# A decoder trunk step: all 576 tokens together against two groups of 288 that pass the layers out of step

## The chip, the cores and the metric

The kernel runs on one core of one Trainium2 chip. A core has TensorE (PE, the matmul array, with PEld for its weight loads), VectorE (DVE), ScalarE (ACT), GpSimd (POOL) and SyncE (SP), which here issues the DMAs. Each engine takes its instructions in program order, and the engines meet through semaphores. The metric is the device time of one execution in microseconds (us).

## The reference

Two layers, each of three sub-layers with a norm before and after, on 512 prompt tokens (one sequence) and 64 sample tokens (8 sequences of 8) that share the weights. Model width 1024, hidden width 2816, all in float32.

```python
def layer(x, ...):
    x = x + 0.5 * rmsnorm(swiglu(rmsnorm(x, pre0), gate0, up0, down0), post0)
    m, h_last, new_conv, S_fin = mixer(rmsnorm(x, pre1), ...)
    x = x + rmsnorm(m, post1)
    x = x + 0.5 * rmsnorm(swiglu(rmsnorm(x, pre2), gate1, up1, down1), post2)

def mixer(h, ...):
    xl, yl, q, k, v, g, gd = split(h @ w_in)
    xc = causal_conv(xl, width 4)                       # carries 3 rows along the sequence
    hl = rg_lru(xc)                                     # h_t = a_t*h_(t-1) + b_t, gates from 64x64 blocks
    lru_out = rmsnorm(hl * gelu(yl), lru_norm)
    gk = log_sigmoid(gd @ w_gate + b) / 16
    o, S = gla(q, k, v, gk)                             # 4 heads, chunks, state S carried on
    gla_out = rmsnorm(o, gla_norm) * silu(g)
    return concat(lru_out, gla_out) @ w_out
```

Outputs are the tokens after two layers, and the recurrence, convolution and attention states of both kinds of sequence.

## The kernel before

Activations lie transposed in SBUF: 128 channels on the partitions, 8 tiles of channels, 576 tokens along a row (`NT`), of which each matmul takes a half of 288 (`H`). A weight matrix is cut into *units*: one output tile of 128 channels with all its inputs, (128 x 1024) for gate, up, w_in and w_out and (128 x 1408) for down, whose 22 input tiles go in two chunks of 11.

Float32 products are made of three passes of the short format fp32r. ACT rounds a weight unit to `wh` (line 624), DVE forms the rest `wl` = raw - wh (line 823), and PE adds wh·xh + wh·xl + wl·xh (line 373). The operands have the same two parts: `hh` and `hl`, or `hidh` and `hidl` for the hidden layer.

There are two slots (0 and 1) of raw, wh and wl and two of PSUM (`psU`). SP loads the next unit into `raw` when DVE is done with the last (`lo_ready`). `out_taken` tells PE that DVE has emptied a slot of PSUM. Every unit does both halves of the tokens, so each weight is loaded from HBM and split once.

A feed-forward sub-layer goes: gate unit, up unit; DVE takes the gate times the norm's factor `rstd` (line 896), ACT makes the silu (693), POOL multiplies by `rstd` (1232), DVE takes the up product times that (904), ACT rounds it to `hidh` (695) and POOL makes `hidl` (1234). After each chunk the 8 down units follow. Sums of squares over the channels are made by ACT (square), POOL (line 1207, `ssum`) and PE, which sums over the partitions in columns (431); ACT takes a root, DVE a reciprocal and a diagonal (840), and PE spreads it over the partitions (439). Then DVE scales the result (873), adds it to x (878) and makes the next `hl` (846), with ACT's `hh` (641) between.

In the mixer, each of 4 tiles of the recurrence takes four units of w_in, with convolution, gates and scan on DVE and ACT between them. Then come 4 chunks of 128 prompt tokens and one of 64 sample tokens of the attention. Chunks follow one another with no unit of a weight between: exponents (DVE 998), keys (DVE 1014), queries (POOL 1244), scores (PE 490 to 500), placing by masks (DVE 1032, 1044), outputs (PE 512, 523), state (PE 529, 539; DVE 1051 to 1065). Then the norms of the mixer (PE 431, 598) and its output as operand (DVE 1123 to 1131, ACT 795, POOL 1287), and w_out.

Each engine's program is written out by hand, with hardware loops over units, tiles, chunks and layers. One thing follows another for all 576 tokens.

Of the kernel before, what the change touches and what calls it, by code (L numbers as in the profile page):

```python
# [39 lines left out]
NTC = NT // TC  # L55
# [10 lines left out]
V_XC, V_D, V_ONE, V_B, V_AH, V_BS, V_A0, V_H, V_O = 4, 5, 6, 7, 8, 9, 10, 11, 12  # L66
A_R, A_I, A_TAU, A_AA, A_L1, A_L2, A_M, A_GE = range(1, 9)
P_HEAD, P_IX, P_ST = 1, 2, 3

G_SC, G_S, G_KEM, G_S1, G_S2 = 1, 2, 2, 3, 4  # L70
D_N, D_E, D_VC = 1, 2, 3
A_VT, A_KET, A_O = 1, 2, 3
T_VT, T_KE, T_SA, T_SB, T_O, T_SU = range(1, 7)


class Tally:

    def __init__(self, small_step=None):  # L80
        self.small_step, self.count, self.open, self.pauses = small_step, {}, [], 0

    def pause(self):


        if self.small_step:
            self.small_step(self.pauses)
            self.pauses += 1

    def now(self, sem, more=0):  # L90
        v = self.count.get(sem.name, 0) + more
        for reg, rises in self.open:
            if rises.get(sem.name, 0):
                v = reg * rises[sem.name] + v
        return v

    def up(self, sem, k=1):
        self.count[sem.name] = self.count.get(sem.name, 0) + k
        return self.now(sem)

    @contextmanager
    def loop(self, eng, times, rises):
        before = dict(self.count)
        with eng.Fori(0, times) as i:
            self.open.append((i, rises))
            yield i
            self.open.pop()
        rise = {k: v - before.get(k, 0) for k, v in self.count.items() if v != before.get(k, 0)}
        assert all(rises.get(k) == v for k, v in rise.items()), f"a loop raises {rise}, said {rises}"
        for k, v in rise.items():  # L110
            self.count[k] = before.get(k, 0) + v * times

# [25 lines left out]
def halves(ap):  # L138
    return ap.rearrange("p (a n) -> p a n", a=2)
# [1253 lines left out]
```

## Time and profile before

| what | us |
|---|---|
| median of the 3 runs shown | 2519.77 |
| the 3 runs | 2513.7, 2519.77, 2522.1 |
| span of the profiled execution, first to last instruction | 2507.5 |
| median less span | 12.3 |
| PE busy | 2306.2 (92%) |
| DVE busy | 1015.1 (40%) |
| ACT busy | 750.0 (30%) |
| POOL busy | 588.7 (23%) |
| mean granted TensorE clock | 0.939 |
| moved by DMA | 180.67 MB, mean 72 GB/s |

The page gives the span of the profiled execution; that execution has no separate time beside it, so the 12.3 us between the span and the median stand for what lies around it. Busy shares are averages over stages. A busy PE is not PE at full rate, since the ends of matmuls are modelled and overlap; the rate is read from a dense stretch, by count.

### The profile page before, as it was taken

How to read it: one execution, taken by the hardware profiler on the slowest of the kernel's cores; microseconds unless marked ns; L12 is line 12 of the kernel's file. 1: busy time of each engine (PE TensorE's matmuls, PEld its weight loads, DVE VectorE, ACT ScalarE, POOL GpSimd, SP SyncE). 2: the span in 40 equal slices, each digit the busy share in tenths (PEclk: the TensorE clock that was granted, in tenths of full speed). 3: DMA queues.
4: the chain of work that ended last, by engine and by line, in shares of the span. 5: the costliest groups of instructions: out<-in, count | busy, mean ns of one | idle time of the engine just before them, and what ended most of it. 6: DMA issues, size and time to landing. Idle time of an engine off the chain costs nothing.

```text
span 2507.5 us, 43035 instructions
## 1 busy us (share of the span) xinstructions
PE 2306.2 (92%) x16980; PEld 2261.6 (90%) x16980; DVE 1015.1 (40%) x1202; ACT 750.0 (30%) x967; POOL 588.7 (23%) x424
## 2 busy tenths in 40 slices
PE   6999999799678999999879999997996879999997
PEld 6999999699577999999879999996985779999997
DVE  4332332655845422233353223326557453322333
ACT  4221222365423321122232212223653232212221
POOL 3220222221222321122222202222112232201221
PEclk9999999899768999999989999998997689999998
DMA  3222222022011222222112222221220112222221
GB/s 127 84 92 68 84 90 80 26 91 84 0 36 67 68 84 93 72 79 91 54 59 84 95 71 78 93 78 35 80 75 3 51 51 77 86 90 75 81 89 63
DMA packets 48604, 180.67 MB, mean 72 GB/s; under 512 B 5617, under 2 KB 7697, under 8 KB 48017
## 3 DMA queue, kind: packets, MB, share of 16 engines
q1 hardware_dynamic: 48528, 179.63, 22.2%
q8 instruction: 52, 0.85, 0.1%
q14 instruction: 24, 0.19, 0.0%
HBM read 174.74 MB, written 4.87 MB: 72 GB/s over the span
## 4 chain that ended last, share of the span: by engine, by line
PE 82%; issue 6%; DVE 5%; POOL 2%; ACT 2%; DVEq 1%; SPq 0%; DMA 0%; ACTq 0%; POOLq 0%
PE psU L373 79%; DVE hl L846 1%; POOL hl L1287 1%; DVE xT L878 1%; POOL ssum L1207 1%; PE psM L439 1%; DVE sc L1032 1%; PE psM L512 1%; DVE dec L998 1%; PE psM L562 1%; PE psM L431 1%; DVE tmp L873 0%; PE psM L523 0%; POOL qf L1244 0%; PE psU L529 0%
## 5 line engine op out<-in xcount | busy, mean ns | idle before, releaser
L373 PE MATMUL psU<-hh,wh 128*128 128x288 f32 x3712 | 815.5, 302 | 82.1 <-DVE hl L846 45.1
L373 PE MATMUL psU<-hh,wl 128*128 128x288 f32 x3712 | 807.1, 300 | 0.0
L373 PE MATMUL psU<-hl,wh 128*128 128x288 f32 x3712 | 806.7, 299 | 0.0
L624 ACT ACTIVATE wh<-raw 128x1024 fp32r<-128x1024 f32 (+1 forms) x296 | 334.4, 1130 | 1261.9 <-PE psU L373 1261.9
L373 PEld LDWEIGHTS psU<-hh,wh 128*128 128x128 f32 x3712 | 610.0, 192 | 97.8 <-issue 72.2
L373 PEld LDWEIGHTS psU<-hh,wl 128*128 128x128 f32 x3712 | 610.4, 192 | 0.0
L373 PEld LDWEIGHTS psU<-hl,wh 128*128 128x128 f32 x3712 | 609.8, 192 | 0.0
L823 DVE TENSOR_TENSOR wl<-raw,wh 128x1024 fp32r<-128x1024 f32 (+1 forms) x296 | 402.9, 1362 | 134.6 <-ACT wh L624 133.8
L1232 POOL TENSOR_TENSOR actr<-act,rstd 128x576 f32<-128x576 f32 x88 | 168.2, 1912 | 664.0 <-ACT act L693 642.2
L373 PE MATMUL psU<-hidh,wh 128*128 128x288 f32 x1408 | 302.3, 296 | 0.0
L373 PE MATMUL psU<-hidl,wh 128*128 128x288 f32 x1408 | 302.2, 296 | 0.0
L373 PE MATMUL psU<-hidh,wl 128*128 128x288 f32 x1408 | 302.1, 296 | 0.0
L1234 POOL TENSOR_TENSOR hidl<-hid,hidh 128x576 f32 x88 | 158.3, 1799 | 396.2 <-ACT hidh L695 389.3
L1207 POOL TENSOR_TENSOR ssum<-ssum,sq 128x576 f32<-128x576 f32 x92 | 152.8, 1661 | 349.1 <-ACT sq L659 155.3
L373 PEld LDWEIGHTS psU<-hidh,wh 128*128 128x128 f32 x1408 | 227.4, 189 | 0.0
L373 PEld LDWEIGHTS psU<-hidl,wh 128*128 128x128 f32 x1408 | 227.4, 188 | 0.0
L373 PEld LDWEIGHTS psU<-hidh,wl 128*128 128x128 f32 x1408 | 227.4, 188 | 0.0
L904 DVE TENSOR_TENSOR hid<-psU,actr 128x576 f32<-128x576 f32 x88 | 66.7, 758 | 351.4 <-PE psU L373 342.3
L896 DVE TENSOR_TENSOR gate<-psU,rstd 128x576 f32<-128x576 f32 x84 | 63.7, 758 | 324.2 <-PE psU L373 324.2
L930 DVE COPY yT<-psU 128x576 f32 (+1 forms) x32 | 24.2, 758 | 189.3 <-PE psU L373 189.3
L932 DVE TENSOR_TENSOR yT<-psU,yT 128x576 f32 (+1 forms) x32 | 24.2, 758 | 173.0 <-PE psU L373 173.0
L846 DVE SCALAR_TENSOR_TENSOR hl<-xT,par,hh (+1 forms) x48 | 69.4, 1478 | 8.2 <-ACT hh L641 8.1
(186 smaller groups left out, 1377.5 us busy)
## 6 DMA issues: line engine op xcount, KB each, us to landing
raw<-in_w_gu SPq DMA_DIRECT2D x176, 512.0 KB, 3.5
raw<-in_w_d SPq DMA_DIRECT2D x64, 704.0 KB, 4.0
raw<-in_w_in SPq DMA_DIRECT2D x40, 512.0 KB, 3.5
raw<-in_w_out SPq DMA_DIRECT2D x16, 512.0 KB, 3.6
yT<-in_xT SPq DMA_DIRECT2D x8, 288.0 KB, 5.0
out_yT<-xT SPq DMA_DIRECT2D x8, 288.0 KB, 2.1
S<-in_st_gla SPq DMA_DIRECT2D x2, 1024.0 KB, 7.5
out_gla_s<-S SPq DMA_DIRECT2D x2, 1024.0 KB, 5.6
```

The source lines that it names most:

```text
L373: mm = e.matmul(out[h], w[:, kt * M:(kt + 1) * M], x[:, kt, h * H:(h + 1) * H], start=(kt == 0 and part == 0), stop=(kt == KT - 1 and part ...
L431: mm = e.matmul(bank[0:TC, at + t:at + t + 1], src[:, t * TC:(t + 1) * TC], means[:, k:k + 1], start=(first and t == 0), stop=last, skip_g ...
L439: mm = e.matmul(psM[:, 1 + h, 0:H], ones[0:TC, :], diag[0][0:TC, 3 * h:3 * h + 3, :], start=True, stop=True)
L512: mm = e.matmul(psM[:, 2 + odd, pr * C:pr * C + T], vt[0:T, h * DV:(h + 1) * DV], (scs if sample else sc)[0:T, 2 * odd + pr, 0:T], start=( ...
L624: e.activation(wh[s][:, 0:width], raw[s][:, 0:width], ACT.Copy).then_inc(hi_ready[s], 1)
L823: e.tensor_tensor(wl[s][:, 0:width], raw[s][:, 0:width], wh[s][:, 0:width].bitcast(F32), ALU.subtract)\
L846: e.scalar_tensor_tensor(tile(hl, m), tile(xT, m), col(par, l * NPAR + (PRE + stage * DT) + m), tile(hh, m).bitcast(F32), ALU.mult, ALU.su ...
L896: e.tensor_tensor(halves(out), psum(s), halves(rstd[:, :]), ALU.mult).then_inc(out_taken[s], 1)
L904: e.tensor_tensor(halves(hid[:, :]), psum(1), halves(actr[:, :]), ALU.mult).then_inc(out_taken[1], 1)
L1207: e.tensor_tensor(ssum[:, :], ssum[:, :], sq[s][:, :], ALU.add).then_inc(sq_used, 1)
L1232: e.tensor_tensor(actr[:, :], act[:, :], rstd[:, :], ALU.mult).then_inc(silur_ready, 1)
L1234: e.tensor_tensor(tile(hidl, j), hid[:, :], tile(hidh, j).bitcast(F32), ALU.subtract).then_inc(hidl_ready, 1)
```

## The change

The 576 tokens become two groups: group 0 has the first 256 prompt tokens and 4 sample sequences, group 1 the other 256 and 4, so 288 tokens each (`T`). Every unit is now done once for each group. Each weight is loaded and split twice in a layer. The hidden layer goes in chunks of 8, 7 and 7 tiles. Within a layer the stages of the two groups alternate:

```python
for l in range(L):
    order += [Stage("ffn", l, 0, 0, c) for c in range(3)]
    order += [Stage("ffn", l, 1, 0, 0), Stage("win", l, 0), Stage("ffn", l, 1, 0, 1), Stage("ffn", l, 1, 0, 2)]
    order += [Stage("wout", l, 0), Stage("win", l, 1), Stage("ffn", l, 0, 1, 0), Stage("ffn", l, 0, 1, 1)]
    order += [Stage("wout", l, 1), Stage("ffn", l, 0, 1, 2)]
    order += [Stage("ffn", l, 1, 1, c) for c in range(3)]
```

Here the arguments are layer, group, which feed-forward, and chunk. That makes 656 units. What lies between units (norms, recurrence, attention) is written as generators with one step in a *slot*; each engine calls `sides.step()` once after each unit, so one step of each live generator lies between two units of a stage. The core of the difference (lines of the new kernel, cut):

```diff
-            for part, (w, x) in enumerate([(w_h, xh), (w_h, xl), (w_l, xh)]):
-                for h in (0, 1):
-                    mm = e.matmul(out[h], w[:, kt * M:(kt + 1) * M], x[:, kt, h * H:(h + 1) * H],
+            e.wait_ge(lo_ready, u + 1)
+            if u >= BANKS:
+                e.wait_ge(out_taken, u - BANKS + 1)
...
+                for part, (w, t) in enumerate([(w_h, xh), (w_h, xl), (w_l, xh)]):
+                    mm = e.matmul(out, w[:, kt * P:(kt + 1) * P], t[:, kt, :],
...
+RING, BANKS = 6, 3
+HI_AHEAD, LO_AHEAD = 4, 3
+CHUNKS = (8, 7, 7)
+T_EXPONENTS = (0, 8, 16)
+T_KEYS = (5, 13, 18)
...
+    raw_at = cursor[0]
+    raw = [sb(f"raw{s}", [P, D]) for s in range(RING)]
+    cursor[0] = raw_at
+    wl = [sb(f"wl{s}", [P, D], F32R) for s in range(RING)]
...
+                    if u >= RING:
+                        e.wait_ge(unit_done, u - RING + 1)
+                    e.dma_start(raw[u % RING][:, 0:depth(u) * P], a[name][at, :, :]).then_inc(raw_landed[u % RING], 16)
...
+        def boundary(l, st, g, timing, final):            # vector
+            start, end, at_once = timing
+            for slot in range(end + 3):
+                if slot == start + 1:
+                    inverse_ready()
+                    diagonal(0)
+                if slot == start + 2:
+                    keep_rstd(rpost)
+                m = (slot - start - 3) * at_once
...
+                        e.scalar_tensor_tensor(tmp[t % 2][:, :], y[g][:, t, :], col(ph, l * 24 + st * DT + t), rpost[:, :],
...
+                m = (slot - start - 5) * at_once
...
+                        operand_lo(l2_, st2, g, t)
...
+            e.tensor_tensor(inv[:, 0:width], cols[:, 0:width], minus_half[:, 0:width], ALU.pow).then_inc(inv_ready, 1)   # gpsimd
...
+                        e.tensor_tensor(x[g][:, t, :], x[g][:, t, :], tmp[t % 2][:, :], ALU.add).then_inc(x_ready[g], 1)   # gpsimd
...
+    def pace(s):
+        if s.kind == "ffn" and s.f == 0 and s.g == 1:
+            return 0, 8, 2
+        if s.kind == "wout" and s.g == 0:
+            return 4, 18, 1
+        return 1, 15, 1
...
+            if s is not STAGES[0]:                        # vector, scalar, gpsimd
+                sides.finish(g)
...
+                    take(u, gate[:, :], rstd[g][:, :])
+                    lo(u + LO_AHEAD)
+                    sides.step()
```

So PE may run three units ahead of DVE's taking, DVE makes `wl` three units ahead, in the place of `raw`, and a load goes out when the unit six before it is done. The boundary between two sub-layers (`pace` gives its first slot, its last and how many channel tiles in a slot) is: PE's sums in slot `start`, DVE's diagonal one later, PE's spread and DVE's `rpost` two later, then x in slots from `start` + 3, and the sums of the next norm in slot `end`. The root is now POOL's `pow`, the addition to x and the exponents of the attention go from DVE to POOL, and no hardware loops are left. A stage first finishes what is live of its own group (`sides.finish`), on DVE, ACT and POOL. The convolution's rows, the recurrence's last value and the attention state S go from group 0 to group 1. The attention of a group has 2 chunks of 128 and one of 32 tokens.

PE in one unit. Before, in the first units, each weight (`wh`, `wl`) serves two matmuls, of the two halves:

```order
L373 MATMUL psU<-hh,wh_54 128x288 x2
L373 MATMUL psU<-hl,wh_54 128x288 x2
L373 MATMUL psU<-hh,wl_56 128x288 x2
L410 REGISTER_ALU
```

After, a weight serves one matmul; the row of `psS` behind the first unit is the sum of squares of group 0, and the next its spread:

```order
L402 MATMUL psD<-hh_51,wh_59 128x288
L402 MATMUL psD<-hl_52,wh_59 128x288
L402 MATMUL psD<-hh_51,wl_71 128x288
...
L408 MATMUL psS<-means,ssum_84 96x1 x3
L427 MATMUL psS<-diag_90,ones 128x288
L402 MATMUL psD<-hh_51,wh_60 128x288
```

The same matmuls of 288 columns are split over two passes through the units.

PE in the attention. Before, a chunk of 128 tokens stands whole, from the transposes to the state, inside a loop:

```order
L475 MATMUL psU<-ident,vc 128x128 x4
L479 MATMUL psU<-ident,kf 128x128 x2
L490 MATMUL psM<-qf,kf 128x64 x16
L497 MATMUL psM<-qf,kf 128x128
L500 MATMUL psM<-qf,kf 128x64
L512 MATMUL psM<-sc,vt 128x128 x4
L523 MATMUL psM<-qe,S 128x128 x4
L529 MATMUL psU<-vt,ket 64x128 x4
```

After, units of the other group's feed-forward stand between the steps (two units where the first "..." stands, four where the last one stands; one row of them is shown):

```order
L535 MATMUL psM<-ident,qkv 128x128 x4
L539 MATMUL psM<-ident,kf_131 128x128 x2
L402 MATMUL psD<-hh_53,wh_59 128x288
...
L510 MATMUL psM<-qf,kf_131 128x64 x16
L516 MATMUL psM<-qf,kf_131 128x128
L519 MATMUL psM<-qf,kf_131 128x64
...
L559 MATMUL psM<-sc,vt_132 128x128 x4
L570 MATMUL psM<-qe_150,S 128x128 x4
L580 MATMUL psM<-vt_132,ket_133 64x128 x4
```

The small matmuls keep their order; dense ones have come between.

DVE at the end of w_out of group 0 and the start of w_in of group 1, layer 0. `y_55` is the result of group 0, `tmp` and `hl_54` belong to group 1's boundary, `rstd_82` is group 1's factor, `xlp` its first taken unit:

```order
L1252 COPY y_55<-psD 128x288
L900 TENSOR_TENSOR wl_75<-raw_69,wh_63 128x1024
L929 SCALAR_TENSOR_TENSOR hl_54<-x_50,par,hh_53 128x288 x4
L913 TENSOR_TENSOR diag_90<-ident,inv 96x288
L923 COPY rstd_82<-psS 128x288
L1233 TENSOR_TENSOR xlp<-psD,rstd_82 128x256
L1234 TENSOR_TENSOR xlp<-psD,rstd_82 128x4x8
L900 TENSOR_TENSOR wl_76<-raw_70,wh_64 128x1024
L991 TENSOR_SCALAR cv_127<-xlp,par 128x300
```

Before, at this place, the factor is kept once for all tokens, and the same steps of the recurrence are twice as wide:

```order
L840 TENSOR_TENSOR diag_73<-ident,dinv 96x576
L861 COPY rstd<-psM 128x576
L1076 TENSOR_TENSOR gd<-tmp_78,rstd 16x576
L945 TENSOR_TENSOR xlp<-psU,rstd 128x288
L946 TENSOR_TENSOR xlp<-psU,rstd 128x224
L947 TENSOR_TENSOR xlp<-psU,rstd 128x8x8
L952 TENSOR_SCALAR cv_111<-xlp,par 128x600
```

The boundary of group 1 now stands in DVE's queue between the last units of w_out of group 0 and the first taken unit of w_in of group 1.

## Rows read from the trace of the kernel before

**Rows 1.** The page, span and part 1: busy us, share, instructions

```profile
span 2507.5 us, 43035 instructions
PE 2306.2 (92%) x16980; PEld 2261.6 (90%) x16980; DVE 1015.1 (40%) x1202; ACT 750.0 (30%) x967; POOL 588.7 (23%) x424
```

**Rows 2.** The page, part 2: granted TensorE clock in 40 slices

```profile
PEclk9999999899768999999989999998997689999998
```

**Rows 3.** The chain of waits in order of time: start us, us, what

```profile
42.94 409.60 PE psU L373 x3072
...
486.06 1.96 PE psM L431 x24
...
528.13 1.94 PE psM L562 x8
```

**Rows 4.** PE's groups, shapes apart: operation, operands, count | busy, mean ns

```profile
L373 PE MATMUL psU<-hh,wh 128*128 128x288 f32 x3712 | 815.5, 302 | 82.1 <-DVE hl L846 45.1 <-ACT hh L641 20.9 <-POOL hl L1287 15.2
...
L373 PE MATMUL psU<-hidh,wh 128*128 128x288 f32 x1408 | 302.3, 296 | 0.0
...
L373 PE MATMUL psU<-hh,wgdh 128*16 128x288 f32 x32 | 8.2, 346 | 22.8 <-DVE hl L846 22.4
```

**Rows 5.** Timeline of PE in the attention of layer 0: start us, us, instructions

```profile
651.95 0.82 PE L475 MATMUL psU<-ident,vc 128*128 128x128 f32 x4
...
655.48 0.38 PE L500 MATMUL psM<-qf,kf 64*128 64x64 f32 x4
661.41 2.08 PE L512 MATMUL psM<-sc,vt 128*128 128x128 f32 x8 [5.55 <-DVE sc L1044]
...
665.62 0.81 PE L475 MATMUL psU<-ident,vc 128*128 128x128 f32 x4
...
693.95 4.58 PE L523 MATMUL psM<-qe,S 64*128 64x8 f32 x63
...
699.67 7.09 PE L539 MATMUL psM<-vt,kem 64*64 64x128 f32 x64
```

**Rows 6.** Stretches, L373 alone: us, PE busy (count), PEld busy, clock, DMA share, GB/s

```profile
0.00:42.90 42.90, 17.41 (x97) 16.00 (x98) 0.96 0.44 149
```

**Rows 7.** Timeline, last sums of squares before the end

```profile
2485.44 1.14 PEld L431 LDWEIGHTS psM<-means,ssum 128*96 128x96 f32 x12
```

**Rows 8.** DVE's groups, shapes apart

```profile
L823 DVE TENSOR_TENSOR wl<-raw,wh 128x1024 fp32r<-128x1024 f32 x232 | 298.1, 1285 | 78.6 <-ACT wh L624 77.9 <-issue 0.7
...
L1014 DVE TENSOR_TENSOR kf<-dec,qkv 128x1792 f32<-128x1792 f32 x8 | 25.2, 3152 | 0.0
...
L954 DVE SCALAR_TENSOR_TENSOR cv<-xlp,par,cv 128x600 f32<-128x600 f32 x8 | 6.8, 844 | 1.3 <-DVE cv L952 1.3
...
L945 DVE TENSOR_TENSOR xlp<-psU,rstd 128x288 f32<-128x288 f32 x8 | 3.6, 453 | 10.9 <-PE psU L373 10.9
...
L960 DVE SCALAR_TENSOR_TENSOR xc<-xlp,par,cv 128x64 f32<-128x64 f32 x8 | 2.2, 280 | 0.0
```

**Rows 9.** ACT's groups, shapes apart

```profile
L624 ACT ACTIVATE wh<-raw 128x1024 fp32r<-128x1024 f32 x232 | 246.1, 1062 | 938.9 <-PE psU L373 938.9
...
L731 ACT ACTIVATE oT<-psM 128x256 f32 x12 | 4.0, 381 | 30.0 <-PE psM L523 30.0
```

**Rows 10.** POOL's groups, shapes apart

```profile
L1232 POOL TENSOR_TENSOR actr<-act,rstd 128x576 f32<-128x576 f32 x88 | 168.2, 1912 | 664.0 <-ACT act L693 642.2 <-ACT act L687 21.8
...
L1287 POOL TENSOR_TENSOR hl<-l,hh 128x576 fp32r<-128x576 f32 x16 | 22.4, 1402 | 38.2 <-ACT hh L795 38.2
...
L1248 POOL TENSOR_TENSOR qe<-qkv,eb 128x256 f32 x6 | 4.3, 724 | 11.6 <-PE psM L523 11.6
```

**Rows 11.** Timeline of DVE and POOL at the mixer's values

```profile
721.75 0.52 DVE L1129 TENSOR_SCALAR l<-tmp,par 128x576 f32<-128x576 f32 x1 [0.15 <-DVE tmp L1123]
...
723.07 1.40 POOL L1287 TENSOR_TENSOR hl<-l,hh 128x576 fp32r<-128x576 f32 x1 [5.30 <-ACT hh L795]
723.09 1.69 DVE L1129 TENSOR_SCALAR l<-tmp,par 128x576 f32<-128x576 f32 x1 [0.15 <-DVE tmp L1123]
```

**Rows 12.** The page, parts 3 and 6: DMA share, and a load's time to landing

```profile
q1 hardware_dynamic: 48528, 179.63, 22.2%
...
raw<-in_w_gu SPq DMA_DIRECT2D x176, 512.0 KB, 3.5
```

More of the change, by code:

```diff
@@ L16 @@
-from contextlib import ExitStack, contextmanager
+from contextlib import ExitStack
 import concourse.bass as bass
@@ L64 @@
 O_CP, O_CS, O_HP, O_HS, NST = 0, 3, 27, 28, 36
[L66 to L111, printed above, removed]
@@ new lines, in depth, with __init__, start, step @@
+def depth(u):
+    name = SOURCES[u][0]
+    return CHUNKS[int(name[3])] if name.startswith("w_d") else DT
+class Sides:
+    def __init__(self):
+        self.live = []
+    def start(self, g, work):
+        self.live.append((g, work))
+    def step(self):
+        self.live = [(g, work) for g, work in self.live if next(work, "end") != "end"]
+    def finish(self, g):
+        while any(own == g for own, _ in self.live):
+            mine = [(own, work) for own, work in self.live if own == g]
+            over = [work for _, work in mine if next(work, "end") == "end"]
+            self.live = [(own, work) for own, work in self.live if not any(work is o for o in over)]
@@ L305, in _, with operand_round @@
+    def operand_round(s):
+        f = {"win": 1, "ffn": 2 * s.f}[s.kind]
+        return DT * (3 * s.l + f + 1)
     @block.sync
     def _(e):
-        n = Tally()
-        def load(s, width, src):
-            e.wait_ge(lo_ready[s], n.now(lo_ready[s]))
-            n.up(lo_ready[s])
-            e.dma_start(raw[s][:, 0:width], src).then_inc(raw_landed[s], 16)
-        def pairs(times, width, src, first):
-            with n.loop(e, times, PAIR) as j:
-                for s in (0, 1):
-                    load(s, width, dram(src, first + j * 2 + s))
@@ L466, in decays_next @@
[L466 to L482 removed]
+        sides = Sides()
@@ L616, in _ @@
+        for g in range(G):
+            sides.finish(g)
     @block.scalar
     def _(e):
[L618 to L630 removed]
@@ L816, in _ @@
+        for g in range(G):
+            sides.finish(g)
     @block.vector
     def _(e):
[L818 to L827 removed]
@@ L892, in take, with lo @@
-        def take(s, out, scale=None):
-            product_done(s)
+        sides = Sides()
+        steps = Steps(e, dve_step)
+        event = [0]
+        kept = [0]
+        diags = [0]
+        tmps = [0, 0]
+        def lo(u):
+            if u < UNITS:
+                width = depth(u) * P
+                e.wait_ge(hi_ready, u + 1)
+                e.tensor_tensor(wl[u % RING][:, 0:width], raw[u % RING][:, 0:width], wh[u % RING][:, 0:width].bitcast(F32),
+                                ALU.subtract).then_inc(lo_ready, 1)
@@ new lines, in root, with diags_before, first_norm @@
+        def root(width):
+            event[0] += 1
+            e.wait_ge(cols_kept, event[0])
+            if event[0] > 1:
+                e.wait_ge(diag_ready, diags_before(event[0]))
+            e.tensor_tensor(inv[:, 0:width], cols[:, 0:width], minus_half[:, 0:width], ALU.pow).then_inc(inv_ready, 1)
+        made = [0]
+        sizes = []
+        def diags_before(n):
+            return sum(sizes[:n - 1])
+        def first_norm(g):
+            for m in range(DT):
+                add_square(g, m)
+                if g:
+                    yield
+            sizes.append(1)
+            root(NTC)
+            yield
```

2079 lines of the change are left out of this document (1132 added, 947 removed).

## The prediction, made before the changed kernel was run

> **What bounds the kernel now.** I read the page's busy shares first, then the clock by slices, then the chain of waits, then groups and timelines. PE is busy 92% of a span of 2507.5 us, and no other engine over 40% [rows 1]. The clock falls only in two groups of slices (and a little at the ends of sub-layers) [rows 2]: these are the places where PE waits. The chain shows the rest as unbroken stretches: 3072 matmuls in 409.60 us, which is 133.3 ns each [rows 3]. No other engine can make that stretch shorter.
>
> The counts give the floor. Three passes of 3712 and of 1408 matmuls [rows 4] are 15,360, at 133.3 ns 2048.0 us, and the three passes of 32 for the low-rank map 12.8 us, together 2060.8. The other 446.7 us of the span are what a change of order can touch: lead, tail, small matmuls, and waits in boundaries and in the attention, where for instance one chunk's outputs wait 5.55 us for DVE's placing [rows 5].
>
> **What stays: the dense work.** The changed kernel issues 24 matmuls of 288 columns for a unit, 656 units less a kt in 128 of them: again 15,360. A weight served two matmuls in turn and each had its own load; now it serves one. So 2060.8 us again, and a unit of 24 takes 3.20 us.
>
> **Small matmuls, at full clock.** They move between units and cost PE their own time whatever covers them.
> - Gates of the recurrence: 4 in 1.94 us [rows 3], 0.485 each. There are 32 of the same width, 15.5 us, and 8 of the logits, 3.9.
> - Spreads: 24 for norms and boundaries and 5 for each of 4 mixers, 44: at 0.485, 21.3 us (96 partitions in place of 128, same columns).
> - Columns: 12 in 1.96 us [rows 3], 0.163 each; 24 sums of 3 and 4 mixers of 24 are 168, 27.4 us.
> - Attention: a chunk of 128 took 651.95 to 655.86 and 661.41 to 665.62 [rows 5], 8.1 us, times 8: 65. A sample chunk had 32 state matmul pairs in 4.58 and 32 updates in 7.09 us at the low clock [rows 5]; a group has half of them, and half of that again at the full clock for the second: about 7.5 with the rest, times 4: 30.
>
> Sum 163 us. Floor 2060.8 + 163 = 2224.
>
> **Lead and tail.** At 42.90 us 96 of the dense matmuls are done (97 in the count) [rows 6], worth 12.8: a lead of 30.1. Only 288 tokens stand before the first norm now, but with one `sq` buffer: ACT's square (256 wide 0.38, 1024 wide 1.06 [rows 9], so 0.42) and POOL's addition alternate, 1.6 with DVE's `hl` between, 8 times after about 13 us for the loads and the first weights, and 2.5 for the norm: PE goes on at about 27, having done one unit: a lead of 24. From the last sums (2485.44) to the end of the span 22.1 us are left [rows 1, 7]; for 288 tokens tmp 0.5 plus POOL's addition 0.8 in turn, 8 times, and the norm and the store: 18. So 2224 + 24 + 18 = 2266.
>
> **What each engine does per unit.** For DVE, 256 to 288 columns from PSUM take 453 ns, a two-input step in SBUF lies between 280 (64 wide) and 844 ns (600 wide), so 0.50 at 288; `wl` 1.285 [rows 8]. DVE: 1.285 + 0.453 = 1.74 of 3.20 us. ACT: 1.062 for `wh` and 0.42, 1.48. POOL: 724 ns at 256 wide, 1402 at 576, 1912 where DVE works beside it [rows 10]; I take 0.80 at 288, bounds 0.72 and 1.40. DVE and ACT thus double their weight work and still fit below a unit. DMA: 656 loads are 335 MB, 144 GB/s over the span, so its share of 22.2% goes to about 45%. A load lands 3.5 us after issue [rows 12] and has two units (6.4 us) and more before ACT reads it: nothing, and at twice the landing time 7.0 a few tenths at most. POOL's `pow` is shown by no row; it has 3 or 15 columns. Below, nothing (it takes the place of ACT's root and DVE's reciprocal); above, the 1.40 us of a 576-wide POOL step. Its slot has 3.2 us, so I take nothing, 24 times 1.4 = 34 us at most.
>
> **Where DVE and POOL meet.** The timeline has a scale by DVE in 0.52 us, and the same one in 1.69 us when a POOL step of 1.40 runs beside it [rows 11]: they followed each other. So in full slots I add POOL's steps to DVE's steps that read SBUF.
>
> The Trainium skill ("SBUF — State Buffer", section "SBUF: two separate sides") says that the pair of ports shared by the two is an exclusive lock held for the whole instruction, also against a DVE step with two SBUF inputs. Rows 11 agree for the one-input step. It speaks against this change, which doubles `wl` and gives POOL the additions and exponents; if it didn't hold, the places below would cost next to nothing and the time would be that of the first rival.
>
> - w_out of group 0 and w_in of group 1, 28 units. PE needs 28 x 3.2 + 10 = 100 us. The pair needs 28 x 1.13 for `wl` (its unhindered value), two boundaries of 8 x (0.5 + 0.5 + 0.8 + 0.8) = 41.6, squares of the output 5.6, recurrence about 21, forget gates 3: 103. So 3 us too much, and badly spread, with two tiles in a slot in w_out. Then comes the order: DVE finishes group 1's boundary before it takes w_in's first unit. Its `hl` are 3 us late for PE; and `rstd` waits for PE's spread after the third unit, whose gates wait in the same place for `xc`. Behind the spread DVE has three takes, two `wl`, the convolution: 0.45 + 0.66 + 1.29 + 1.65 + 0.45 + 1.29 + 0.75 = 6.5 us in which PE stands. With the clock that it loses about 16 us, in 2 layers: 32.
> - Seven boundaries beside a feed-forward: a slot asks 1.13 + 4 steps of the boundary 2.6 + POOL's 0.8 = 4.5 of 3.2 us for six slots, 8 too much. Three units of `wl` ahead hide up to 4.8, so I take 2 each (0 to 5): 14.
> - Eight chunks of 128: keys and queries are 1.58 (3152 for twice the width [rows 8]) and 1.77 in two slots, 4.2 us too much, and the transposes follow one slot later: 1.5 each (0 to 4): 12.
> - Last hidden tile before the down units, 24 times: take, round, `hidl` are 0.45 + 0.42 + 0.80 and three hand-overs, about 2.2, and PE asks for it 2.4 to 2.8 after the unit. 0.3 each: 7.
>
> Sum 65 us. Span 2266 + 65 = 2331. The median stands 12.3 over the profiled span now: **2343 us**, 7% below 2519.8.
>
> **The rivals.**
> *All hidden.* The slack of three units swallows the overloads, and the waits are 20 us: 2286 + 12 = 2298. For it: DVE needs 1.74 of 3.20 us. Against: rows 11, and the in-order wait for `rstd`.
> *The pair of DVE and POOL holds PE back locally.* Upper bounds: 7 x 6 + 8 x 4 for boundaries and chunks, 70 for the two stretches at w_in, 20 for the tiles: 165, so 2431 + 12 = 2443. For it: POOL's 1912 beside 1402 ns. Against: it loses only where both have work queued.
> *Slower: DVE, blocked by every POOL step, sets the pace of the whole kernel.* Then DVE's queue is the clock: `wl` 656 x 1.285 = 843, takes 656 x 0.453 = 297, boundaries, recurrence, keys and the rest about 383, in all 1523 us, plus all of POOL. POOL has 664 steps of 288 columns and 130 us of others. At 0.80 that is 661 and the sum 2184, below the floor; if a narrow step kept the price of a wide one, 1.40, POOL has 1060, the sum is 2583, and with lead and tail 2625 + 12 = 2637. It decides from 1.22 us per POOL step on. Against: 724 ns at 256 wide.
> *The change doesn't do what it says.* If the two groups did not overlap, the waits of now would come twice, at half the width: no gain. The order of rows shows the units of one group between the other's steps, so I give this nothing of its own.
>
> **How the numbers follow.** My forecast (waits of 45 to 110 us, 2320 to 2390) 50%; all hidden 24%; locally held back 20%, some of it above 2443; the slow case 5%, and no change 1%. About 0.3% is what a measurement can tell from no change. So faster 0.94, same 0.01, slower 0.05. The range runs from 2285 (all hidden, cheaper small matmuls) to 2440: 1.5 in 10 above, under 1 in 10 below.
>
> **What would show it.** Dense stretches at 133 ns per matmul and clock 1.0 nearly everywhere, and a PE idle share of under 5% between lead and tail: right. The attention's PE steps with no idle before them. DVE busy about 1400, ACT 1200, POOL 700 us. POOL's 288-wide step at 0.8 to 0.95 us; above 1.2 the slow case is on. PE's longest waits in the first three units of w_in of group 1, released by DVE's `xc` or `hl`. If PE waits for `wl` in every unit, or for `raw` landing, my terms per unit are wrong; if lead and tail are not 24 and 18, those.

## The result: 2398.9 us, 4.7% below before

| | before | after | forecast |
|---|---|---|---|
| median of the runs of one chip | 2520.2 | 2398.9 | 2343 |
| lowest and highest (4 runs each) | 2513.7, 2522.1 | 2391.4, 2401.4 | range 2285 to 2440 |
| span of the profiled execution | 2507.5 | 2389.6 | 2331 |
| granted TensorE clock, mean | 0.939 | 0.970 | "1.0 nearly everywhere" |

The ratio is 0.9527, 95% interval 0.9503 to 0.9551. Sign and range held. Of the forecast gain of 177 us, 121 came, so the time lies 56 us above the forecast, 44 us below the rival of 2443, and outside the 2320 to 2390 that I gave my own account. The profiled execution is the fastest of the four.

The page of the kernel after, its span and parts 1 and 2, where the slices of the clock answer to [rows 2], and then its DMA queue [rows 12]:

```profile
span 2389.6 us, 40752 instructions
...
PE 2270.2 (95%) x16960; PEld 2231.4 (93%) x16960; DVE 1428.6 (60%) x1961; ACT 1111.6 (47%) x1657; POOL 936.7 (39%) x961
...
PEclk9999999989899999999999999999989999999998
...
q1 hardware_dynamic: 102064, 348.00, 45.8%
...
raw<-in_w_gu SPq DMA_DIRECT2D x352, 512.0 KB, 3.6
```

DVE came out at 1429 us (forecast 1400), ACT at 1112 (1200), POOL at 937 (700). The DMA share doubled and a load lands as fast as before. The deep dips of the clock in the middle of each layer have gone, and shallow ones have stayed. By the granted clock of the trace, the time at the lower of the two levels fell from 305 to 144 us.

What PE waits for in the kernel after (releaser: us in total, times, longest us):

```profile
PE psD L402 <- DVE hl L929: 29.7, 11, 15.8
PE psM L486 <- DVE xc L1004: 25.7, 6, 5.8
PE psM L535 <- DVE S L1095: 13.9, 8, 2.2
PE psS L408 <- POOL ssum L1274: 10.8, 6, 2.1
PE psD L402 <- POOL hidl L1474: 10.2, 4, 4.7
PE psM L539 <- DVE kf L1060: 5.8, 4, 1.5
PE psM L510 <- issue: 5.7, 2, 2.8
PE psS L427 <- DVE diag L913: 3.6, 2, 1.8
PE psD L402 <- DVE wl L900: 2.2, 1, 2.2
```

No entry for a landing load, and one for `wl`: the work per unit fits. The 15.8 us are the start. Of these 107.6 us, 23.7 stand at the two ends, and 83.9 between them.

The groups of DVE and POOL in the kernel after that carry the terms (columns as in [rows 8, 10]):

```profile
L900 DVE TENSOR_TENSOR wl<-raw,wh 128x1024 fp32r<-128x1024 f32 x528 | 664.2, 1258 | 9.4 <-ACT wh L670 9.4
...
L959 DVE SCALAR_TENSOR_TENSOR tmp<-y,ph,rpost 128x288 f32<-128x288 f32 x96 | 87.2, 918 | 2.1 <-POOL x L1309 2.0
```

```profile
L1471 POOL TENSOR_TENSOR actr<-act,rstd 128x288 f32<-128x288 f32 x176 | 209.5, 1191 | 511.5 <-ACT act L855 511.5
...
L1274 POOL TENSOR_TENSOR ssum<-ssum,sq 128x288 f32<-128x288 f32 x168 | 201.2, 1199 | 205.1 <-ACT sq L679 205.1
L1309 POOL TENSOR_TENSOR x<-x,tmp 128x288 f32<-128x288 f32 x96 | 90.9, 952 | 64.8 <-DVE tmp L959 64.8
...
L1281 POOL TENSOR_TENSOR inv<-cols,minus_half 96x3 f32<-96x3 f32 x24 | 23.8, 994 | 49.4 <-ACT cols L686 49.4
```

**The span taken apart.** Every matmul is given the time to the start of the next. What exceeds 0.6 us and three times its line's median counts as a wait, less the median. "Dense" are the matmuls of 288 columns with the low-rank map. The columns add up to the span (e0_after is the kernel after, run again and profiled in an execution of median time):

| us | dense at 133.3 ns | dense above that | small matmuls | waits | before first, after last matmul | span |
|---|---|---|---|---|---|---|
| before | 2060.7 | 43.7 | 187.7 | 178.6 | 36.8 | 2507.5 |
| after | 2060.7 | 60.1 | 137.3 | 103.1 | 28.4 | 2389.6 |
| e0_after | 2060.7 | 66.9 | 140.2 | 101.4 | 27.7 | 2396.9 |
| e1_order | 2060.7 | 39.7 | 224.3 | 175.4 | 28.1 | 2528.2 |
| e2_wl_narrow | 2060.7 | 48.4 | 139.7 | 50.1 | 28.0 | 2326.9 |
| e6_x_on_dve | 2060.7 | 57.1 | 140.1 | 93.1 | 27.2 | 2378.2 |
| e8_x_pace | 2060.7 | 57.1 | 140.0 | 91.6 | 27.2 | 2376.5 |
| e9_fat_cols | 2060.7 | 63.6 | 134.7 | 102.7 | 28.1 | 2389.8 |
| e10_actr | 2060.7 | 45.5 | 138.3 | 92.9 | 27.0 | 2364.4 |
| e11_best | 2060.7 | 40.2 | 132.7 | 92.2 | 26.5 | 2352.3 |

"Dense above that", laid beside the granted clock of the trace, has three parts. After, 366 dense matmuls start while the clock is at its lower level, most of them 0.24 to 0.27 us apart in place of 0.133: 41.3 us. At the full clock, the first dense matmul behind small ones takes 0.2 to 0.35 us to the next: 104 of these cost 15.4 us, and other short stalls 3.5. Before, the three parts are 35.5, 4.0 and 4.2 us. From before to after, waits fell by 75 us, small matmuls by 50 and the ends by 8, and the dense work rose by 16: 118 us.

Two executions of one and the same kernel differ by 7 us in span here (after, e0_after), nearly all of it in the two columns of matmuls; differences of that size between two single profiles say little.

### The profile page after: what moved, and what is told of

Read it like the earlier page. It is cut to its first block, busy times and chain, and to the rows that moved or that the text cites. A ratio compares the mean times of both kernels' runs of the same rounds, so it can differ in the third digit from the quotient of the medians.

```text
span 2389.6 us, 40752 instructions
## 1 busy us (share of the span) xinstructions
PE 2270.2 (95%) x16960; PEld 2231.4 (93%) x16960; DVE 1428.6 (60%) x1961; ACT 1111.6 (47%) x1657; POOL 936.7 (39%) x961
## 3 DMA queue, kind: packets, MB, share of 16 engines
q8 instruction: 135, 2.21, 0.4%
## 4 chain that ended last, share of the span: by engine, by line
PE 83%; POOL 7%; DVE 5%; issue 3%; ACT 1%; DMA 0%; SPq 0%; POOLq 0%; DVEq 0%
PE psD L402 76%; POOL ssum L1274 3%; POOL x L1309 2%; DVE wl L900 2%; PE psS L408 1%; DVE kf L1060 1%; PE psM L486 1%; POOL hidl L1474 1%; POOL actr L1471 1%; PE psM L510 1%; PE psS L427 1%; PE psM L570 1%; PE psM L466 1%; PE psM L559 0%; DVE tmp L959 0%
## 5 line engine op out<-in xcount | busy, mean ns | idle before, releaser
L402 PE MATMUL psD<-hh,wh 128*128 128x288 f32 x3712 | 1131.5, 305 | 31.9 <-DVE hl L929 29.7
L402 PE MATMUL psD<-hl,wh 128*128 128x288 f32 x3712 | 1109.5, 299 | 0.0
L402 PE MATMUL psD<-hh,wl 128*128 128x288 f32 x3712 | 1105.3, 298 | 0.0
L900 DVE TENSOR_TENSOR wl<-raw,wh 128x1024 fp32r<-128x1024 f32 (+1 forms) x656 | 806.3, 1229 | 10.6 <-ACT wh L670 10.6
L402 PEld LDWEIGHTS psD<-hh,wh 128*128 128x128 f32 x3712 | 710.4, 191 | 43.7 <-issue 18.7
L402 PEld LDWEIGHTS psD<-hl,wh 128*128 128x128 f32 x3712 | 711.6, 192 | 3.1
L402 PEld LDWEIGHTS psD<-hh,wl 128*128 128x128 f32 x3712 | 712.8, 192 | 0.0
L402 PE MATMUL psD<-hidh,wh 128*128 128x288 f32 x1408 | 424.0, 301 | 10.2 <-POOL hidl L1474 10.2
L402 PE MATMUL psD<-hidl,wh 128*128 128x288 f32 x1408 | 419.5, 298 | 0.0
L402 PE MATMUL psD<-hidh,wl 128*128 128x288 f32 x1408 | 418.8, 297 | 0.0
L1471 POOL TENSOR_TENSOR actr<-act,rstd 128x288 f32<-128x288 f32 x176 | 209.5, 1191 | 511.5 <-ACT act L855 511.5
L1274 POOL TENSOR_TENSOR ssum<-ssum,sq 128x288 f32<-128x288 f32 x168 | 201.2, 1199 | 205.1 <-ACT sq L679 205.1
L1219 DVE TENSOR_TENSOR y<-psD,y 128x288 f32<-128x288 f32 x128 | 58.6, 458 | 164.4 <-PE psD L402 164.3
```

Of the source, the lines that this page charges most:

```text
L402: mm = e.matmul(out, w[:, kt * P:(kt + 1) * P], t[:, kt, :], start=(kt == 0 and part == 0), stop=(kt == KT - 1 and part == 2))
L900: e.tensor_tensor(wl[u % RING][:, 0:width], raw[u % RING][:, 0:width], wh[u % RING][:, 0:width].bitcast(F32), ALU.subtract).then_inc(lo_re ...
L1219: e.tensor_tensor(y[g][:, m, :], bank(u), y[g][:, m, :], ALU.add).then_inc(out_taken, 1)
L1274: e.tensor_tensor(ssum[g][:, :], ssum[g][:, :], sq[g][:, :], ALU.add).then_inc(sq_used[g], 1)
L1471: e.tensor_tensor(actr[:, :], act[:, :], rstd[g][:, :], ALU.mult).then_inc(actr_ready, 1)
```

## The experiments

Ratios are to the kernel before, run beside them on the same chip, with 95% intervals. Its medians were 2513.9 us beside e1 to e4, 2518.5 beside e0, e5, e6 and e7, and 2516.1 beside e8 to e11, three chips. The kernel after, run once more beside the second group, is the yardstick:

> The changed kernel again, beside the next three on one chip: 0.95 to 0.955 of the kernel before, as in its first measurement (0.9527).

It took 2398.7 us, ratio 0.9534 [0.9516, 0.9551].

**e1_order: the groups no longer out of step in the attention.**

```diff
-        order += [Stage("ffn", l, 0, 0, c) for c in range(3)]
-        order += [Stage("ffn", l, 1, 0, 0), Stage("win", l, 0), Stage("ffn", l, 1, 0, 1), Stage("ffn", l, 1, 0, 2)]
-        order += [Stage("wout", l, 0), Stage("win", l, 1), Stage("ffn", l, 0, 1, 0), Stage("ffn", l, 0, 1, 1)]
-        order += [Stage("wout", l, 1), Stage("ffn", l, 0, 1, 2)]
-        order += [Stage("ffn", l, 1, 1, c) for c in range(3)]
+        order += [Stage("ffn", l, 0, 0, c) for c in range(3)] + [Stage("ffn", l, 1, 0, c) for c in range(3)]
+        order += [Stage("win", l, 0), Stage("wout", l, 0), Stage("win", l, 1), Stage("wout", l, 1)]
+        order += [Stage("ffn", l, 0, 1, c) for c in range(3)] + [Stage("ffn", l, 1, 1, c) for c in range(3)]
```

(and `pace` of w_out of group 0 as elsewhere, 1, 15, 1)

> The same groups, units, steps and straight-line code, but the stages stand so that nothing covers the attention: in each layer both groups' first feed-forwards, then w_in and w_out of group 0, w_in and w_out of group 1, then the second feed-forwards (and the boundary behind w_out of group 0 has the pace 1, 15, 1). If the gain comes from units of the other group between the steps of the attention: each of four attentions is bare again, some 45 to 60 us each, so 2570 to 2640 us, above the kernel before. If it comes from straight-line code, the narrower lead and tail and the covered boundaries: under 2450 us.

Measured: 2529.9 us, ratio 1.0058 [1.0034, 1.0083]. The page's clock and PE's longest waits in e1_order:

```profile
PEclk9999999986976999999999999999679679999998
```

```profile
PE psM L537 <- DVE kf L1058: 47.8, 4, 12.0
PE psS L425 <- DVE diag L911: 27.0, 8, 4.9
PE psM L484 <- DVE xc L1002: 22.5, 6, 4.7
PE psM L557 <- DVE sc L1084: 20.4, 8, 3.7
```

The dips of [rows 2] are back, each now in two, one for each group. Waits for `kf` and `sc`, nearly absent after, come to 68 us. So with everything else of the change in place (smaller groups, deeper rings, POOL's share) and only the order of the stages changed, the kernel is slightly slower than before. All of the gain lies in that order: 131 us by the medians. The two profiles differ by 138.6: 72 of waits and 87 of small matmuls, which in e1_order run alone and mostly at the low clock (184 of their 224 us), less 20 that the dense work pays. The time is in neither of the two expected ranges: the order costs 131 us and not 170 to 240, so some 33 us for each attention and not 45 to 60. That some boundaries still lay beside a feed-forward may be the reason, and wasn't tested; nor was the attention's order changed alone, since the boundaries and recurrences moved with it.

**e2_wl_narrow: DVE's work per unit nearly gone.** It subtracts only 128 of a unit's 1024 columns, and PE's third pass multiplies `wh` in place of `wl`; the low part of the weights is left out, PE's work is the same.

```diff
-    wl = [sb(f"wl{s}", [P, D], F32R) for s in range(RING)]
+    wl = wh
...
+                width = P
-                e.tensor_tensor(wl[u % RING][:, 0:width], raw[u % RING][:, 0:width], wh[u % RING][:, 0:width].bitcast(F32),
+                e.tensor_tensor(raw[u % RING][:, 0:width], raw[u % RING][:, 0:width], wh[u % RING][:, 0:width].bitcast(F32),
```

> Leaves out a part of the computation: DVE subtracts only 128 of 1024 columns of each weight unit, and the third pass of PE reads wh in place of wl, so DVE keeps its steps and order and loses about 0.95 us of each. If the waits come from too much work for DVE and POOL together in full slots: the waits between lead and tail (83 us) fall to 35 or less and with them half of the time at the low clock, 2335 to 2350 us. If they come from the order in which the engines hand over, whatever their load: over 2385 us.

Measured: 2332.2 us, ratio 0.9278 [0.9254, 0.9302], 67 us below the kernel after and 3 below the expected range; waits 103 to 50 (between the ends 83.9 to 35.6), the time at the low clock 144 to 117 us, which is less than the half that was expected to go. POOL's groups in e2_wl_narrow, and DVE's `tmp`:

```profile
L1472 POOL TENSOR_TENSOR actr<-act,rstd 128x288 f32<-128x288 f32 x176 | 151.5, 861 | 579.1 <-ACT act L855 579.1
...
L1275 POOL TENSOR_TENSOR ssum<-ssum,sq 128x288 f32<-128x288 f32 x168 | 140.0, 835 | 231.7 <-ACT sq L679 231.7
```

```profile
L960 DVE SCALAR_TENSOR_TENSOR tmp<-y,ph,rpost 128x288 f32<-128x288 f32 x96 | 53.2, 564 | 2.1 <-POOL x L1310 2.0
```

POOL's instructions are the same as after and nothing was taken from POOL, but `actr` fell from 1191 to 861 ns and `ssum` from 1199 to 835. So `wl` stretches POOL's steps by more than a third. The shorter `wl` is worth about 50 us of waits; how much of that is DVE's own time and how much POOL's, this run doesn't separate. My 0.80 was POOL's price with DVE quiet.

**e3_slow_pace: boundaries beside a feed-forward with one tile in two slots.**

```diff
+        if s.kind == "wout":
+            return 1, 15, 1
-        return 1, 15, 1
+        return 1, 21, 0.5
```

> The boundaries beside feed-forward stages of group 0's first and both groups' second sub-layer take one channel tile in two slots instead of one (pace 1, 21, 0.5); work and amounts are the same. If the load of DVE and POOL in a slot makes the waits: five of seven such waits (2.1 to 4.7 us each) go, POOL's additions fall from the chain there, 2380 to 2388 us. If handing over makes them, each tile costs the same wait: 2395 to 2405 us.

Measured: 2388.9 us, ratio 0.9494 [0.9472, 0.9516]. PE's waits for `ssum` went from 10.8 to 2.0 us, the others stayed. That is 8 to 10 us by the ratios, about as much as that wait; the interval only just touches that of e0_after. So the overloaded slots of the boundaries cost about what PE waited in them.

**e4_split_cols: 12 of the 24 column sums in a mixer's norms go to four earlier slots, 3 in each.**

```diff
-                if slot == T_SUMS:
-                    sums_free()
-                    e.wait_ge(lru_squared, i + 1)
-                    for t in range(LT):
-                        columns(squares[g][:, t, :], 1, 0, t == 0, True, t == LT - 1)
+                for t, at in enumerate((24, 25, 27, 28)):
+                    if slot == at:
+                        if t == 0:
+                            sums_free()
+                            e.wait_ge(lru_squared, i + 1)
+                        columns(squares[g][:, t, :], 1, 0, t == 0, True, t == LT - 1)
```

> The 12 one-column matmuls for the squares of the recurrence's output go from the slot with the heads' 12 to four earlier slots, 3 in each. If the 24 one-column matmuls in a row (4.9 us) are what lowers the clock behind them: the low stretches of 6.8 us behind them go or shrink to 3.4, 4 times 1.5 to 2.2 us, 2390 to 2394 us. If the matmuls of the sample chunk a few units earlier do it: no change, 2397 to 2401 us.

Measured: 2393.8 us, ratio 0.9519 [0.9496, 0.9543], which cannot be told from 0.9527. The stretch at the low clock behind the columns halved in three of the four mixers and went in the fourth. The one behind the sample chunk, which stands in the neighbouring slots, grew to twice its length or more in three. Inconclusive: the low clock was mostly moved, not removed.

**e5_shift: the recurrence of group 1 two slots later, for the wait for `xc`.**

```diff
         def recurrence(s):
+            for _ in range(2 * g):
+                yield
```

(two on PE, ACT and DVE, one on POOL)

> The steps of group 1's recurrence come two units later on PE, ACT and DVE and one later on POOL; all else is the same. If PE stands at w_in of group 1 because its gates follow directly behind the spread of rstd, before DVE has worked off three units: the waits of PE for xc (25.7 us, 6 times) fall by half or more, 8 to 16 us less than the changed kernel, ratio to it 0.993 to 0.997. If DVE's and POOL's amount of work in these 28 units sets it: the wait moves to another place (wl or out_taken) and the time stays within 3 us.

Measured: 2402.4 us, ratio 0.9542 [0.9527, 0.9556]: nothing gained. The waits in e5_shift:

```profile
PE psM L488 <- DVE xc L1010: 15.7, 4, 4.0
...
PE psM L541 <- DVE kf L1066: 10.7, 4, 3.9
...
PE psD L402 <- DVE wl L904: 6.7, 3, 2.2
```

The wait for `xc` fell by 10.0 us, and those for `kf` and `wl` rose by 4.9 and 4.5. A later start moved the wait and didn't save it. That DVE has the same queue before the same place fits this, but wasn't tested by itself.

**e6_x_on_dve: x + tmp by DVE, directly behind `tmp`, in place of POOL.**

```diff
                         e.scalar_tensor_tensor(tmp[t % 2][:, :], ..., ALU.mult, ALU.mult).then_inc(tmp_ready[g], 1)
+                        e.wait_ge(tmp_ready[g], done + t + 1)
+                        e.tensor_tensor(x[g][:, t, :], x[g][:, t, :], tmp[t % 2][:, :], ALU.add).then_inc(x_ready[g], 1)
```

> The addition to x goes back from POOL to DVE, as in the kernel before. POOL's step took 0.95 us, DVE's takes 0.45 to 0.70. If DVE and POOL share one resource in the full slots, the sum counts and falls by 0.3 us in 96 places: 5 to 15 us less than the changed kernel. If DVE alone is the bound there: 5 to 20 us more, with the waits at w_in of group 1 growing.

Measured: 2382.2 us, ratio 0.9464 [0.9449, 0.9479], 16.5 us below the kernel after. From e6_x_on_dve, DVE's new group and PE's wait for `ssum`:

```profile
L962 DVE TENSOR_TENSOR x<-x,tmp 128x288 f32<-128x288 f32 x96 | 60.4, 630 | 3.3
```

```profile
PE psS L408 <- POOL ssum L1276: 3.0, 5, 2.0
```

The same addition takes 630 ns on DVE and took 952 on POOL, and giving the busier engine more work made the kernel faster. That isn't what a load counted by engine would say. The edit also saves a hand-over from DVE to POOL, but in the chain of the kernel after that is 0.07 us in the last tiles; 96 of them would be 7 us at most, if all were on PE's path.

**e7_all: e3, e4 and e5 together** (its shift two slots on PE, ACT and DVE, one on POOL).

> Slower boundaries beside feed-forwards, the split columns, and group 1's recurrence later, together. If the places are independent: the gains add, 8 (slower boundaries) + 2 (columns) + 8 to 16, so 15 to 25 us less than the changed kernel. If the waits only move on to the next place: 8 to 10 us less.

Measured: 2380.0 us, ratio 0.9457 [0.9441, 0.9474]: 19 us below e0_after. By the ratios e3 and e4 give 10 and 4 us, so this is about their sum, and e5 adds nothing that can be told.

**e8_x_pace: e3 and e6 together.**

> The two edits that each took something off the changed kernel, together: x = x + tmp by VectorE (alone -16.5 us) and the boundaries beside the feed-forwards at one tile in two slots (alone -9). If they relieve different waits, the gains add: 2369 to 2378. If both only removed the same wait of PE for POOL's ssum (10.8 us before, 3.0 and 2.0 behind them), nothing is added: 2380 to 2386. A third way: VectorE's in-order wait for tmp now stands in slots where it had slack, and hl comes later: above 2386.

Measured: 2378.3 us, just between the two expected ranges. By the ratio, 0.9465 [0.9437, 0.9493], it is the same as e6 alone (0.9464), on another chip. Waits are 91.6 against 93.1 in e6, and both edits alone had removed nearly the same wait for `ssum`. So nothing added is the better reading, though the interval would hide a few us.

**e9_fat_cols: the sums of squares by matmuls of 48 columns, 47 of them zeros.**

```diff
-                mm = e.matmul(psS[0:TC, 0, 288 + at + t:289 + at + t], src[:, t * TC:(t + 1) * TC], means[:, k:k + 1],
+                mm = e.matmul(psS[0:TC, 0, 288 + at + t:336 + at + t], src[:, t * TC:(t + 1) * TC], means[:, k, :],
```

> Each sum of squares uses a 48-column matmul (47 columns of zeros) in place of one of one column; same count, same results, nothing else moved. If the clock falls behind these matmuls because PE does too little in them, the low periods behind the columns of the mixers go, the excess of slow dense starts (53.7 to 58.5 us) falls by 8 to 15 and the time by 5 to 10 us, to 2388 to 2394. If the clock only follows the waits of PE, nothing changes: 2396 to 2402. If the 48 columns are not hidden below the weight load, 168 of them cost up to 0.08 us each, 13 us: 2402 to 2412.

Measured: 2391.6 us, ratio 0.9497 [0.9468, 0.9526]. In time alone this doesn't stand apart from 0.9527, and the expected fall of 8 to 15 us in the dense excess didn't show in the whole: 63.6 against 60.1 and 66.9 in the two profiles of the kernel after. The timelines of PE show what happens at one place. The profile has every one of these float32 matmuls twice, so 48 stand for the 24 sums of a mixer. The kernel after, with the stretch's length, PE's and PEld's busy time and the granted clock (1.00 or 0.50) from the view of windows:

```profile
826.58 2.12 PE L408 MATMUL psS<-means,squares 128*96 128x1 f32 x24
828.56 3.09 PE L408 MATMUL psS<-means,qkv 128*96 128x1 f32 x24
...
831.90 0.44 PE L402 MATMUL psD<-hl,wh 128*128 128x288 f32 x1
832.14 0.44 PE L402 MATMUL psD<-hh,wl 128*128 128x288 f32 x1
```

```profile
826.60:829.50 2.90, 2.90 (x38) 2.90 (x36) 1.59 (x2) 1.44 (x3) 1.23 (x1) 1.00 0.48 185
829.60:831.60 2.00, 2.00 (x15) 2.00 (x14) 0.00 (x0) 0.00 (x0) 0.00 (x0) 0.50 0.01 2
```

And e9_fat_cols, the same place:

```profile
831.42 2.16 PE L408 MATMUL psS<-means,squares 128*96 128x48 f32 x24
833.42 2.20 PE L408 MATMUL psS<-means,qkv 128*96 128x48 f32 x24
...
835.66 0.29 PE L402 MATMUL psD<-hl,wh 128*128 128x288 f32 x1
835.79 0.29 PE L402 MATMUL psD<-hh,wl 128*128 128x288 f32 x1
```

```profile
835.50:842.00 6.50, 6.50 (x51) 6.50 (x50) 3.08 (x4) 1.67 (x3) 4.81 (x3) 1.00 0.27 78
```

After, the second 24 take 3.09 us in place of 2.1, the granted clock goes to 0.50 while they run, and the dense starts behind them stand 0.24 us apart, with no wait of PE from 810 to 860 us. With 48 columns they take 2.20, the clock stays at 1.00, and the dense starts stand 0.13 apart. All four mixers show the same: after, the 48 take 4.8 to 5.0 us and the 48 dense matmuls behind them 8.6 to 8.8; in e9_fat_cols 4.02 and 6.47 each time. So here the clock fell at narrow matmuls and not behind a wait, and wider ones in the same number kept it up at no cost. These places add up to 12 us. That less came out in the whole is probably because the low stretches elsewhere differ from execution to execution: they come to 144 and 157 us in the two profiles of the kernel after, and to 136 in e9.

**e10_actr: e8, and silu times rstd by DVE as well.**

```diff
-                    e.wait_ge(actr_ready, hidden + j + 1)
+                    e.wait_ge(silu_ready, hidden + j + 1)
+                    e.tensor_tensor(actr[:, :], act[:, :], rstd[g][:, :], ALU.mult).then_inc(actr_ready, 1)
+                    e.wait_ge(actr_ready, hidden + j + 1)
+                    if hidden + j:
+                        e.wait_ge(hidl_ready, hidden + j)
                     take(u + 1, hid[:, :], actr[:, :])
```

> e8_x_pace, and silu times rstd by VectorE (directly before it takes the up product) in place of POOL: 176 steps of 1.19 us leave POOL, 176 of 0.5 to 0.65 come to VectorE, whose busy time rises to about 1550 us and POOL's falls to about 600. If what is short is the time of the pair, each exchange frees about 0.5 us where both are full, ssum and hidl run in 0.9 to 1.0 us in place of 1.18, and the waits for hidl and ssum go: 2355 to 2368. Rival: VectorE now waits in order for ScalarE's silu in every tile, wl and the side steps behind it come later, and PE waits for hl, xc and S: 2375 to 2400.

Measured: 2372.7 us, ratio 0.9433 [0.9406, 0.9460], between the two expected ranges. A group of DVE and one of POOL in e10_actr:

```profile
L1215 DVE TENSOR_TENSOR actr<-act,rstd 128x288 f32<-128x288 f32 x176 | 90.7, 515 | 0.1
```

```profile
L1475 POOL TENSOR_TENSOR hidl<-hid,hidh 128x288 fp32r<-128x288 f32 x176 | 216.0, 1227 | 1046.9 <-ACT hidh L865 1046.9
```

The step is 515 ns where POOL took 1229 in e8, and POOL has 614 us. But `hidl` stayed at 1227 ns (1212 in e8), where I had expected 0.9 to 1.0, and the waits stayed at 93 us. The 12 us less of span are in "dense above" (57.1 to 45.5). Of these, 10 are dense matmuls at the low clock (36.8 to 26.7 us; the low clock's whole time goes from 141 to 115 us), so short waits for `hidl` are not the cause. What kept the clock up is open. The intervals of e8 and e10 overlap, so the edit's gain isn't shown.

**e11_best: e10 and e9 together.**

> e10_actr and the 48-column sums together. If the effects are independent, e10's time less what e9 gained: 2347 to 2362. If the columns bring nothing or cost, e10's time or up to 10 us more.

Measured: **2359.7 us**, ratio 0.9387 [0.9360, 0.9413], which beats both kernels: 6.1% below before, and below the kernel after outside both intervals. The page of e11_best:

```profile
span 2352.3 us, 40758 instructions
...
PE 2244.5 (95%) x16960; PEld 2208.6 (94%) x16960; DVE 1481.5 (63%) x2233; ACT 1113.1 (47%) x1657; POOL 613.2 (26%) x692
...
PEclk9999999999899999999999999999999999999999
```

On one chip its five runs (2354.1 to 2365.1) lie below all five of e10 (2366.1 to 2376.5). The only difference is the width of the sums, and the time at the low clock falls from 115 to 82 us. In e10 the 48 dense matmuls behind a mixer's columns take 7.8 to 8.6 us, in e11_best 6.47 at all four. So the columns' part in the clock is shown, at 7 to 13 us for the 168 sums of the kernel.

## Why the prediction held, and where it was off

The sign and the mechanism were right: PE sets the end, the attention's waits go, the other engines keep up with a unit. Term by term, against the span of 2331:

**Dense at full clock, 2060.8: the step that failed.** I wrote "So 2060.8 us again" and let the clock come back nearly everywhere. The count is right, 15,360. The chain has 1467 of them at 133.4 ns in a row, but 366 start at the lower level elsewhere, 41 us too much, and the first dense matmul behind small ones costs 15 us more in 104 places at the full clock (why is open); with other stalls it is 60. I had only a few us for that inside the 16 at w_in:

```profile
826.74 4.91 PE psS L408 x48
831.65 8.68 PE psD L402 x48
...
2173.49 195.71 PE psD L402 x1467
```

Before had 44 us of it already, which I could have read: 409.60 us for 3072 [rows 3] was the best stretch, not the mean. The change took 81 us of small matmuls out of the low clock (102 to 21 us), but the dense work's loss there rose a little (35.5 to 41.3 us) instead of going, and changing between small and dense so often added 11 us.

**Small matmuls, 163: 137.** The chunks of the attention cost 69 us and not 95, since [rows 5] had pieces at the low clock and short stalls in them; spreads 14 and not 21; columns 32 and not 27, slowed as shown by e9. This hid nearly half of the miss above.

**Lead 24, tail 18: 25.5 and 20.4.** In the chain the dense stretch starts at 28.75 us with one unit done before. At the end the last dense matmul ends at 2369.2 of 2389.6, and each last tile takes 2.1 us, since `tmp` and `x` are there at 1.04 and 1.01, not 0.5 and 0.8.

**Waits of 65: 84.** The view of waits has 107.6; less 23.7 at the two ends (17.7 for `hl` at the start, 3.6 for `diag`, 2.4 for `ssum`) it is 83.9.
- w_in of group 1, forecast 32: 37.7. Both named places are there, `hl` (6.0 a layer) and `xc` (12.9 a layer):

```profile
PE psM L486 <- DVE xc L1004: 12.9, 3, 5.8
PE psD L402 <- DVE hl L929: 6.0, 3, 3.1
```

  (of 587 to 700 us). The single wait of 5.8 us stands for my 6.5.
- Boundaries and last tiles, forecast 14 + 7 = 21: 20.8 (`ssum` 8.4, `hidl` 10.2, `wl` 2.2). The overload of a slot, forecast 4.5 of 3.2 us, is 4.2 by the chain of group 1's first boundary:

```profile
281.82 1.75 POOL ssum L1274
...
286.04 1.75 POOL ssum L1274
...
290.25 1.75 POOL ssum L1274
```

- Attention, forecast 12: 25.4. Keys and queries cost 5.8 of the 12 (`kf`), but I had left out DVE's update of the state `S` (13.9, eight times up to 2.2 us) and 5.7 us before the scores that the view puts down to issue, twice up to 2.8.

Sum: dense +60, small -26, waits +19, lead and tail +4, together +57, where the span has +58.6. The terms that were most off, dense and small, have opposite signs, so the total was luckier than its parts. With small matmuls as forecast the time would have come to about 2425, still inside the range but near its end.

**The 12.3 us between span and median.** In every run after this, the time is only 1.8 to 1.9 us above the span. The 12.3 were mostly a profiled execution of the kernel before that was faster than the median. In the kernel after, the same difference is 9.3 us (its profile is its fastest run), so this term came out near by luck.

**The 1.13 us for `wl` in full slots.** No run shows it as the price of a 1024-wide step: the fastest took 1.21 us both before and after, and the mean was 1.285 and 1.26. It makes the forecast's overloads a little too small, 2.5 us over 28 units.

**The pair of DVE and POOL.** The in-order wait and the shared time, rivals and forecast alike, rested on [rows 11]. Here is the same in the kernel after, with two inputs to DVE's step:

```profile
281.15 1.75 DVE L900 TENSOR_TENSOR wl<-raw,wh 128x1024 fp32r<-128x1024 f32 x1 [0.68 <-ACT wh L670]
281.77 1.80 POOL L1274 TENSOR_TENSOR ssum<-ssum,sq 128x288 f32<-128x288 f32 x1
```

Alone, POOL's step takes 0.81 (in the lead); `wl` takes 1.21 at best and 1.26 on average. Beside one another the two steps take 1.80 and 1.75. The Trainium skill ("SBUF — State Buffer", section "SBUF: two separate sides") has an exclusive lock between the two, for two-input steps as well. e2's 861 against 1191 ns for an unchanged POOL step agrees.

**The rivals.** *All hidden* (2298) fell with e2: even with `wl` almost gone the time is 2332. *Held back locally* (2443) has the same mechanism as my own account, with more of it. The time, 2398.9, is nearer to it than to my 2343; the waits, 84 us, are nearer to my 65 than to its 165. *DVE sets the pace* was to decide at 1.22 us per POOL step. The step came to 1.19, above the 0.8 to 0.95 that I had named as the sign of being right, and nothing of the kind happened. The busy times of the pair after, 1429 + 937 = 2366, nearly fill the span, but each step's duration contains its wait for the other. In e11_best the sum is 2095, and the time fell by 39 us only. Busy sums of two engines with a shared resource count the wait twice and are no pace; my sum for that rival did so too, by pricing `wl` at 1285 beside a whole POOL. *Does not do what it says* is refuted by the time itself, and by e1, where the overlap is taken away.

## What to carry to other kernels

When a latency-bound part is filled with dense work of an independent half, the gain is its waits plus the clock that its small matmuls win, less what the dense work between them loses. Price the dense work by the mean of a stretch like the one to come, not by the best. Where DVE and POOL both work in SBUF, try giving a step to the engine that holds it shorter, even if that engine is the busier one: it gave 16.5 us for one step here, and nothing clear of noise for a second. A wait behind a full queue may only move when its start is shifted, as in e5; here it shrank when work left the queue, as in e2.

## What the runs showed of the hardware that I had not expected

- The granted clock fell at one-column matmuls with PE never waiting: 48 in the profile in 4.91 us, the last ones at 0.50, then 48 dense ones in 8.68 us in place of 6.4. With 48 columns each, the 48 took 4.02 us and the dense work went on at 133 ns, at all four mixers. The columns were free and kept the level.
- At the full clock, the first dense matmul behind small ones took 0.2 to 0.35 us to the next in place of 0.133, 104 times in the kernel after.
- POOL's 288-wide addition is 0.81 us alone, 1.75 to 1.80 beside a 1024-wide `wl`; DVE does the same addition in 0.50 (e10, e11) to 0.63 (e6) on average.
- `pow` on POOL, unpriced in the forecast, takes 0.99 us for 3 columns. PE's wait for what follows it (`diag`) shows up at the two ends only, 3.6 us of at most 34.
- The program without hardware loops shows no wait for instructions: its instruction queue moved 2.21 MB in 135 packets, and no entry in the view of PE's waits names it.
